# A hybrid decoder layer: decay sums by a scan instead of products, regrouped masked products, and 512-column products in the feed-forward part

## Chip, core, metric

One core of one Trainium2 chip runs the whole layer. The metric is the device time of one execution in microseconds (us). Before the change the median of 3 runs is 466.96 us (466.77 to 468.04).

## What is computed

The layer has one batch of 256 tokens and 1024 channels, all in fp32. Cut to what matters:

```python
h = rms_norm(x, norm1_g);  proj = h @ w_in                 # 1024 -> all mixers and gates
# mixer A (RWKV-7, 8 heads x 64); p is the token-shifted part of proj
w_log = -softplus(-(w0 + tanh(xw) @ w_up)) - 0.5
decay = exp(-exp(w_log))                                   # = exp(-exp(-0.5) * sigmoid(w0 + ...))
a = sigmoid(a0 + xa @ a_up)
kk = heads(k * k_k);  kk = kk / max(norm(kk), 1e-12)       # norm over the 64 channels of a head
k = k * (1 + (a - 1) * k_a)
def step(S, (r, w, k, v, -kk, kk*a)):                      # 256 steps, S is 64 x 64 per head
    sa = S @ a_t
    S = S * w_t + outer(sa, b_t) + outer(v_t, k_t)
    return S, S @ r_t
# group norm, bonus sum(r*k*r_k)*v, gate g; mixer B: causal attention; mixer C: causal pooling
x = x + sum(gates * branch, axis=2) @ w_out
h2 = rms_norm(x, norm2_g)
x = x + square(relu(h2 @ w_ff1)) @ w_ff2                   # 1024 -> 4096 -> 1024
```

The recurrence is computed in blocks: products of decayed keys, queries and values inside a block, the inverse of a triangular matrix by levels of doubling, and a state that is carried from block to block. The factors exp(+sum) and exp(-sum) of the running sums of log decay are what turns the step-wise decay into such products.

## The kernel before

**Units and slots.** All large products are cut into 69 units (`UNITS`, lines 57 to 68), and every engine runs one loop over slots t = 0 to 68, unit t being computed in slot t. A unit has two weight pieces of 128x1024 elements (`PIECES` = 138, piece v belongs to unit v // 2). "feat" units (0 to 6, 13, 14) and "ff1" units have channels on the output's partitions: weights stationary, activations moving, 256 columns (tokens) a product. "tok", "branch", "out" and "ff2" units have tokens on partitions and move 512 columns of weights. From slot 37 on ff1 and ff2 units alternate, 16 of each.

**fp32 by halves.** Each operand is a high part (type fp32r) and a rest, and a product is three (`mm3`, lines 496 to 499): high x high (L497), then the two mixed ones (L498, L499). In a feat or ff1 unit these are 16 x 3 products of 256 columns.

**The weight pipeline.** SyncE (SP) loads piece v into one of 3 stages (L470) once DVE has finished low(v - 3). ScalarE (ACT) casts it to the high part, high(v) (L900), once PE has used piece v - 6. VectorE (DVE) subtracts, low(v) (L1142). PE waits for low(v). `split_places` gives the pieces to the slots: slot 2 has 7, 8 and 9; slot 3 has 10 and 11; slot 4 has 12, 13 and 14; slot 5 has 15 and 16; slot 6 has 17 and 18; slot 7 has 19 and 20; slot 8 has 21 and 22; slot 9 has 23 and 24.

**Order inside a slot.** A slot has four parts p on PE; after part p of the unit PE runs `extra(t, p)`, the small products placed at (t, p). ACT and DVE run their own extra(t, p) in the order 0 to 3 between the high(v) or low(v) of the slot, then `finish(t)` (the unit's result out of PSUM) before extra(t, 3). On ACT slot 3 begins with extra(3, 2). Each engine's order is fixed by this text; a wait in one step holds all behind it on that engine. For t < 7, finish(t) mixes each token with its predecessor: ACT L1068, DVE L1401. Unit t of these uses PSUM bank `FEAT_BANK[t]`; unit 6 uses the bank of unit 4, so PE's part (6, 0) waits for DVE's finish(4).

**Decay.** At (2, 1) PE makes z = tanh(xw) @ w_up with tokens on partitions (L647) and the product for a (L652). DVE, first thing in slot 2, adds w0, which was broadcast to all partitions by a load (`decay_input`, L1178). ACT (2, 1) takes four sigmoids of 256 columns for a (L927) and two of 512 for z (L930). At (3, 2) and (4, 0) PE multiplies the sigmoids by a triangular constant `C_CUM` (`cum`, L663), which gives the running sums of a chunk of 128 tokens, taken from its middle; ACT takes exp of them with both signs (L936, L937) into `e_up` and `e_dn`.

**Norms of kk.** DVE (3, 0) multiplies k by k_k (L1185), ACT (3, 2) squares (L941), PE (4, 1) sums over heads (L671), DVE (4, 1) takes the maximum (L1189), GpSimd (POOL) the root (L1472, once per call), ACT (4, 3) spreads it (`kkb`, L944), PE (5, 2) transposes it, DVE (5, 3) multiplies.

**Products and inverse.** DVE (4, 2) makes k2 (L1195, L1197); (5, 2), (6, 0) and (6, 3) multiply keys and queries by the exponentials; (7, 0) ends with `ops_ready`. `PROD_AT` places four groups of masked products: (8, 0) and (8, 2) for chunk 0, (9, 0) and (9, 2) for chunk 1, each 16 pairs of 64x64 tiles on PE (L626, L629), drained with a mask by DVE (L1246, two of 128x512 a group). Then DVE (8, 3) and (9, 3) builds the start of the inverse (L1255, L1261), and PE transposes it, X0, at (9, 1) for chunk 0 and (10, 1) for chunk 1 (L722). The first level of the inverse is PE's (11, 0) (L743). The bonus product (L706) is at (8, 1), drained by DVE (L1237).

**State.** The state is carried over four steps of 64 tokens, `s_bd`; since sums run from a chunk's middle, it is rescaled once, at n == 1 (L1305).

**Feed-forward.** ff1(i) has one PSUM bank with two halves of 256 columns. In its own slot ACT takes Relu (L1097) and Square into the high part `r_hi` (L1101); DVE squares (L1428) and subtracts into `r_lo` (L1431, the helper at L1146). ff2(i) waits for that; it stands two units behind ff1(i).

Of the kernel before, what the change touches and what calls it, by code (L numbers as in the profile page):

```python
# [28 lines left out]
P = 128  # L29
# [9 lines left out]
WINDOWS = (2, 4, 8, 16)  # L39
PAD = 16  # L40
# [4 lines left out]
C_ID, C_BLK, C_CUM, C_BIAS = 0, 128, 256, 386  # L45
# [31 lines left out]
PROD_AT = {(8, 0): (0, 0), (8, 2): (0, 1), (9, 0): (1, 0), (9, 2): (1, 1)}  # L77
# [44 lines left out]
def plan_turns():  # L122
# [14 lines left out]
    for t, u in enumerate(UNITS):  # L137
# [4 lines left out]
        for p in range(4):  # L142
            if p == 0:
# [37 lines left out]
def pe_uses(t, p):  # L181
# [3 lines left out]
    if (t, p) == (3, 2):  # L185
        return [(("cum", 0, 0),), (("cum", 0, 1),)]
    if (t, p) == (4, 0):
        return [(("cum", 1, 0),), (("cum", 1, 1),)]
# [9 lines left out]
    if (t, p) == (8, 1):  # L198
# [3 lines left out]
    if (t, p) in PROD_AT:  # L202
        out += [(("prod", *PROD_AT[t, p], e),) for e in range(2)]
# [35 lines left out]
    if h2_place(t, p) is not None:  # L239
        out += [(("h2", 2 * h2_place(t, p) + i),) for i in range(2)]  # L240
# [3 lines left out]
def dense_ends():  # L244

    ends = {}
    for t, u in enumerate(UNITS):
# [9 lines left out]
        if u[0] == "ff1":  # L257
            ends[("ff", u[1])] = 2 * t + 2
# [6 lines left out]
def build_layer(nc: bass.Bass, x, w_in, w_up, w0, a_up, g_up, pool_w, w_branch, w_out, w_ff1, w_ff2, vecs, consts, out):  # L265
    turn = plan_turns()
    ctx = ExitStack()
    with ctx:
# [3 lines left out]
        def sem(name):  # L272
# [6 lines left out]
        h_hi = sb("h_hi", [P, KD, T], F32R)  # L279
        h_lo = sb("h_lo", [P, KD, T], F32R)  # L280
# [17 lines left out]
        small = sb("small", [P, 96])  # L298
# [10 lines left out]
        sg = big[:, 2].rearrange("p (t n) -> p t n", t=TT)  # L309
# [4 lines left out]
        e_up, e_dn = (flat[:, 4096 + 1040 * i:4096 + 1040 * i + 1032].rearrange("p (c j t) -> p c j t", c=TT, j=PAIRS)  # L314
                      for i in range(2))
# [22 lines left out]
        w0_wide = att[:, 0:512]  # L338
# [6 lines left out]
        e_end, minus_half = small[:, 48:52], small[:, 52:53]  # L345
# [47 lines left out]
        def copied(eng, name):  # L393
# [6 lines left out]
        id_in, vec_in, cst_in, mask_in, small_in, w0_in, g_in, pool_in = (  # L400
            sem(n) for n in ("id_in", "vec_in", "cst_in", "mask_in", "small_in", "w0_in", "g_in", "pool_in"))
# [9 lines left out]
        keep_part, sg_ready = sem("keep_part"), sem("sg_ready")  # L411
# [15 lines left out]
        f_hi, f_ready = sem("f_hi"), sem("f_ready")  # L427
# [35 lines left out]
        def _(sp):  # L463
# [3 lines left out]
            for v in range(PIECES):  # L467
# [27 lines left out]
        def _(pe):  # L495
# [37 lines left out]
            def part(t, p):  # L533
# [6 lines left out]
                if u[0] in ("feat", "ff1"):  # L540
# [1031 lines left out]
```

## Time and profile before

| | us |
|---|---|
| median of 3 runs | 466.96 |
| profiled execution, its own time | 467.01 |
| its span | 465.2 |
| PE busy | 459.6 |
| PE weight loads busy | 397.7 |
| DVE busy | 295.0 |
| ACT busy | 245.8 |

The span is the profiled time between the first and the last instruction of the core; 1.8 us lie around it. PE's records overlap, since a product is drained while the next one begins: the time that a product costs is the distance between two starts, not its own duration. In a timeline row the first column is the start, the second the time till the end of the last record of the row, "x4" says how many records it merges, and the bracket says how long the engine was idle before and what ended that.

### The profile page before, as it was taken

The numbers are of one execution on the slowest core, as the hardware profiler recorded it, in microseconds if no ns is written. First come the engines' busy times: TensorE is split into PE (matmuls) and PEld (weight loads), VectorE is DVE, ScalarE is ACT, GpSimd is POOL, SyncE is SP. The second block draws the span as 40 slices with busy tenths as digits, with TensorE's granted clock in tenths as the row PEclk, the third lists the DMA queues.
The fourth block names the chain that finished last, engine by engine and source line by source line (L and its number), as shares of the span: only waits on it lengthen the run. The fifth ranks groups of instructions, "written<-read, shape, count | busy, mean of one in ns | idle before, by whom it ended". The sixth has DMA issues, their size and how long they took to land.

```text
span 465.2 us, 8736 instructions
## 1 busy us (share of the span) xinstructions
PE 459.6 (99%) x3660; PEld 397.7 (85%) x3660; DVE 295.0 (63%) x405; ACT 245.8 (53%) x370; POOL 33.1 (7%) x41
## 2 busy tenths in 40 slices
PE   8999999999999999999999999999999999999997
PEld 4999986788977778788888889999999999999995
DVE  4675998674564766766778758655555555555542
ACT  5597655646555456566543538444444444444430
POOL 2000100021670001002000000000000000000000
PEclk9999999999999999999999999999999999999999
DMA  7776635533424435445656564655556656565602
GB/s 235 235 231 217 220 96 177 151 122 93 145 87 136 118 110 142 130 159 171 189 185 184 175 193 143 209 184 184 184 189 194 197 184 182 185 182 190 204 10 90
DMA packets 48694, 76.91 MB, mean 165 GB/s; under 512 B 2576, under 2 KB 28944, under 8 KB 48656
## 3 DMA queue, kind: packets, MB, share of 16 engines
q1 hardware_dynamic: 48656, 76.36, 53.1%
q8 instruction: 29, 0.48, 0.4%
q14 instruction: 9, 0.07, 0.0%
HBM read 75.30 MB, written 1.05 MB: 164 GB/s over the span
## 4 chain that ended last, share of the span: by engine, by line
PE 90%; DVE 3%; ACT 2%; DMA 2%; issue 1%; POOL 1%; DVEq 0%; ACTq 0%
PE bank L497 26%; PE bank L498 25%; PE bank L499 25%; DMA stage<-in_w_in 2%; PE bank L606 1%; PE bank L762 1%; PE bank L743 1%; DVE w_lo L1142 1%; PE bank L638 1%; ACT w_hi L900 1%; POOL small L1472 1%; DVE xs L1458 1%; PE bank L626 1%; PE bank L829 1%; PE bank L793 1%
## 5 line engine op out<-in xcount | busy, mean ns | idle before, releaser
L1142 DVE TENSOR_TENSOR w_lo<-stage,w_hi 128x1024 fp32r<-128x1024 f32 x138 | 167.9, 1225 | 89.1 <-ACT w_hi L900 89.1
L900 ACT CAST w_hi<-stage 128x1024 fp32r<-128x1024 f32 x138 | 144.5, 1052 | 109.5 <-PE bank L499 88.6
L497 PE MATMUL bank<-h_hi,w_hi 128*128 128x256 f32 x384 | 109.8, 286 | 0.3 <-DVE h_lo L1386 0.3
L498 PE MATMUL bank<-h_lo,w_hi 128*128 128x256 f32 x384 | 108.6, 283 | 0.0
L499 PE MATMUL bank<-h_hi,w_lo 128*128 128x256 f32 x384 | 108.6, 283 | 0.0
L497 PEld LDWEIGHTS bank<-h_hi,w_hi 128*128 128x128 f32 x384 | 73.6, 192 | 1.6 <-issue 0.8
L498 PEld LDWEIGHTS bank<-h_lo,w_hi 128*128 128x128 f32 x384 | 73.6, 192 | 0.6
L499 PEld LDWEIGHTS bank<-h_hi,w_lo 128*128 128x128 f32 x384 | 73.6, 192 | 0.0
L497 PE MATMUL bank<-w_hi,h_hi 128*128 128x512 f32 x144 | 60.4, 420 | 0.0
L497 PE MATMUL bank<-w_hi,r_hi 128*128 128x512 f32 x144 | 56.4, 392 | 0.0
L499 PE MATMUL bank<-w_hi,h_lo 128*128 128x512 f32 x144 | 56.4, 391 | 0.0
L498 PE MATMUL bank<-w_lo,h_hi 128*128 128x512 f32 x144 | 56.4, 391 | 0.0
L498 PE MATMUL bank<-w_lo,r_hi 128*128 128x512 f32 x144 | 56.2, 390 | 0.0
L499 PE MATMUL bank<-w_hi,r_lo 128*128 128x512 f32 x144 | 56.0, 389 | 0.0
L497 PEld LDWEIGHTS bank<-w_hi,h_hi 128*128 128x128 f32 x144 | 27.0, 188 | 7.7 <-issue 2.4
L499 PEld LDWEIGHTS bank<-w_hi,h_lo 128*128 128x128 f32 x144 | 27.0, 188 | 6.1
L499 PEld LDWEIGHTS bank<-w_hi,r_lo 128*128 128x128 f32 x144 | 27.0, 188 | 5.8
L497 PEld LDWEIGHTS bank<-w_hi,r_hi 128*128 128x128 f32 x144 | 27.1, 188 | 5.2
L498 PEld LDWEIGHTS bank<-w_lo,r_hi 128*128 128x128 f32 x144 | 27.1, 188 | 4.9
L498 PEld LDWEIGHTS bank<-w_lo,h_hi 128*128 128x128 f32 x144 | 27.1, 188 | 4.7 <-issue 0.2
L1472 POOL TENSOR_TENSOR small<-small 128x8 f32<-128x8 f32 (+2 forms) x9 | 15.0, 1676 | 173.7 <-DVE small L1320 69.1
L1097 ACT ACTIVATE mat<-bank 128x512 f32<-128x512 f32 x16 | 9.6, 599 | 30.5 <-PE bank L499 30.5
(231 smaller groups left out, 541.9 us busy)
## 6 DMA issues: line engine op xcount, KB each, us to landing
stage<-in_w_ff SPq DMA_DIRECT2D x64, 512.0 KB, 3.8
stage<-in_w_in SPq DMA_DIRECT2D x54, 512.0 KB, 3.8
stage<-in_w_branch SPq DMA_DIRECT2D x12, 512.0 KB, 4.5
stage<-in_w_out SPq DMA_DIRECT2D x8, 512.0 KB, 4.1
xs<-in_x SPq DMA_DIRECT2D x2, 512.0 KB, 3.9
out<-xs SPq DMA_DIRECT2D x4, 256.0 KB, 2.1
cst<-in_consts SPq DMA_DIRECT2D x1, 608.0 KB, 6.6
att<-in_w SPq DMA_DIRECT2D x1, 256.0 KB, 5.9
```

The costliest lines, as they stand in the source:

```text
L497: pe.matmul(o, lh, rh, start=first, stop=False)
L498: pe.matmul(o, lh, rl, start=False, stop=False)
L499: return pe.matmul(o, ll, rh, start=False, stop=last)
L606: pe.matmul(banks[3][:], flat[:, 0:P], flat[:, 0:512], start=True, stop=True)
L626: ins = pe.matmul(o[halves[e], P * i:P * i + P], bk[c][halves[e], j, s, 0:HD], ar[c][halves[e], j, :, HD * s:HD * s + HD], start=True, sto ...
L638: ins = pe.transpose(o[:, P * j:P * j + P], x_c[:, c, j].rearrange("p s n -> p (s n)"), ident)
L743: ins = pe.matmul(both[e][halves[s], HD * i:HD * i + HD], gm[c][halves[e], j, s, e, 0:HD], x_c[halves[e], c, j, s], start=True, stop=True)
L762: ins = pe.matmul(both[s][halves[e], HD * i:HD * i + HD], left, right, start=True, stop=True)
L900: nc.scalar.copy(w_hi[:, v % RING], stage[:, v % STAGES]).then_inc(hi_done, 1)
L1097: nc.scalar.activation(ffs[i % 2], o[:], ACT.Relu).then_inc(drained_of(("ff", i)), 1)
L1142: dve.tensor_tensor(w_lo[:, v % RING], stage[:, v % STAGES], w_hi[:, v % RING].bitcast(F32), ALU.subtract)\
L1472: pool.tensor_tensor(ap, ap, half.to_broadcast(shape), ALU.pow).then_inc(done, 1)
```

## The change

1. **Decay.** z is made with channels on partitions (four products of 256 columns at (2, 1), interleaved with those for a). w0 is loaded as four columns (`w0_col`, 4-byte elements, ahead of a_up on SP's queue) and added by ACT as the bias of the sigmoid, which writes into segments of 1 + 64 (`SEG`), the first element of each being 0. One `tensor_tensor_scan` on DVE over 1040 elements (`sum_decay`, in slot 3 behind extra(3, 0)) gives the running sums, restarted in every block of 64 tokens. Two exponentials of 1040 on ACT (3, 2), now between high(10) and high(11), replace eight of 258 columns. The products `cum` and `C_CUM` go.
2. **Norms earlier.** ACT squares at (3, 1), first thing in slot 3; DVE takes the maximum at (3, 1), between low(10) and low(11); ACT spreads the root at (4, 0), first thing in slot 4. PE's sum stays at (4, 1).
3. **Products regrouped.** The two groups of a chunk stand together: (8, 2) and (9, 2). The bonus moves from (8, 1) to (10, 0).
4. **State.** With sums per block of 64 the state is rescaled in each of the steps n = 0, 1 and 2 by its own factor.
5. **Feed-forward.** `h_hi` and `h_lo` become one tile `h_two`; high weights times both are one product of 512 columns into a bank of its own half-unit, the rest of the weights times `h_hi` one of 256 into its second half. DVE adds the halves (two `tensor_reduce`), then max(x, 0) * x in one instruction; ACT copies to `r_hi` at (t + 1, 0) and DVE subtracts at (t + 1, 1).
6. ACT clears `zz` at (6, 3) instead of (7, 2).

```diff
-PROD_AT = {(8, 0): (0, 0), (8, 2): (0, 1), (9, 0): (1, 0), (9, 2): (1, 1)}
+PROD_AT = {(8, 2): 0, (9, 2): 1}
+BONUS_AT = (10, 0)
...
                 elif u[0] == "ff1":
-                    use(("ff", u[1]), dense=True)
+                    for j in range(2):
+                        use(("ff", u[1], j), 6 - 2 * (u[1] % 2) + j, dense=j == 1)
...
                     sp.dma_start(lora[0:64, 0], w_up[0]).then_inc(small_in, 16)
+                    sp.dma_start(w0_col, w0[0].rearrange("(j p) -> p j", p=P), allow_slow_non_contiguous=True).then_inc(small_in, 16)
                     sp.dma_start(lora[64:128, 1], a_up[0]).then_inc(small_in, 16)
-                    sp.dma_start(w0_wide, w0[0].partition_broadcast(P)).then_inc(w0_in, 16)
...
+                if u[0] == "ff1":
+                    name = ("ff", u[1], i)
+                    o = room(pe, name) if p < 2 else ps(name)
+                    cols = slice(P * i, P * i + P)
+                    for kk in range(4):
...
+                        pe.matmul(o[:].rearrange("p (s t) -> p s t", s=2), wh[:, kk, cols], h_two[:, :, k],
+                                  start=k == 0, stop=False)
+                        ins = pe.matmul(o[:, T:2 * T], wl[:, kk, cols], h_hi[:, k], start=False, stop=k == KD - 1)
...
-                if (t, p) in ((3, 2), (4, 0)):
-                    c = t - 3
...
-                            ins = pe.matmul(o[:, 256 * jj:256 * jj + 129], sg[:, c, P * j:P * j + P],
-                                            cst[:, C_CUM:C_CUM + 129], start=True, stop=True)
...
                 if (t, p) in PROD_AT:
-                    products(*PROD_AT[t, p])
+                    for g in range(2):
+                        products(PROD_AT[t, p], g)
...
+                            ins = nc.scalar.activation(sg[:, :, j, :, 1:SEG], o[:, T * jj:T * jj + T].rearrange("p (c s t) -> p c s t", c=TT, s=2),
+                                                       ACT.Sigmoid, bias=w0_col[:, j:j + 1])
...
-                if (t, p) == (3, 2):
+                if (t, p) == (3, 1):
                     act.wait_ge(kkraw_ready, 1)
                     nc.scalar.activation(ksq, kkn, ACT.Square).then_inc(ksq_ready, 1)
-                if (t, p) == (4, 3):
+                if (t, p) == (3, 2):
+                    act.wait_ge(cum_ready, 1)
+                    nc.scalar.activation(e_up_all, cum_all, ACT.Exp, scale=-DECAY).then_inc(e_ready, 1)
+                    nc.scalar.activation(e_dn_all, cum_all, ACT.Exp, scale=DECAY).then_inc(e_ready, 1)
+                if (t, p) == (4, 0):
                     act.wait_ge(kk_inv, 1)
...
+                if p == 0 and UNITS[t - 1][0] == "ff1":
+                    i = UNITS[t - 1][1]
+                    act.wait_ge(sq_ready, i + 1)
...
             for t in range(SLOTS):
                 step = (t, 2) in STEP_AT or (t, 3) in STEP_AT
                 if t == 3:
-                    extra(t, 2)
-                if step:
+                    extra(t, 1)
+                if step or t == 4:
                     extra(t, 0)
                 for v in split_places(2 * t):
                     high(v)
-                if not step:
+                if not step and t != 4:
                     extra(t, 0)
                 late = t in (S_OUT - 1, S_FF - 1)
                 if t == 2 or step:
                     extra(t, 1)
+                if t == 3:
+                    extra(t, 2)
                 for v in () if late else split_places(2 * t + 1):
                     high(v)
...
+            def sum_decay():
+
+                dve.wait_ge(seg_ready, 2)
                 for i in range(2):
...
+                    copied(dve, ("z", i))
+                dve.tensor_tensor_scan(cum_all, restart, sg_all, 0.0, ALU.mult, ALU.add).then_inc(cum_ready, 1)
...
-                if (t, p) == (8, 1):
+                if (t, p) == BONUS_AT:
...
+                    for g, e in ((0, 0), (0, 1), (1, 0), (1, 1)):
                         name = ("prod", c, g, e)
...
+                            ins = dve.tensor_tensor(s_bd[rows, :, e], by_pair(o[rows, 0:PAIRS * HD]),
+                                                    e_end[rows, 0, :, 0:1].to_broadcast([HD, PAIRS, HD]), ALU.mult)
...
+                if p == 1 and UNITS[t - 1][0] == "ff1":
+                    i = UNITS[t - 1][1]
+                    b = 2 * (i % 2)
+                    dve.wait_ge(f_hi, i + 1)
...
+                    for j in range(2):
+                        o = take(dve, ("ff", i, j))
+                        dve.tensor_reduce(ffs[i % 2][:, T * j:T * j + T], o[:].rearrange("p (s t) -> p t s", s=2), AX_X, ALU.add)\
+                           .then_inc(drained_of(("ff", i, j)), 1)
...
+                    dve.scalar_tensor_tensor(out=fsq[i % 2], in0=ffs[i % 2], scalar=0.0, in1=ffs[i % 2],
+                                             op0=ALU.max, op1=ALU.mult).then_inc(sq_ready, 1)
...
             for t in range(SLOTS):
-                if t == 2:
-                    decay_input()
                 extra(t, 0)
+                if t == 3:
+                    sum_decay()
                 for v in split_places(2 * t):
                     low(v)
```

## Rows read from the trace of the kernel before

**Rows 1.** The page: busy times, granted clock, costly groups (L606 from the groups by line).

```profile
PE 459.6 (99%) x3660; PEld 397.7 (85%) x3660; DVE 295.0 (63%) x405; ACT 245.8 (53%) x370; POOL 33.1 (7%) x41
...
PEclk9999999999999999999999999999999999999999
...
L900 ACT CAST w_hi<-stage 128x1024 fp32r<-128x1024 f32 x138 | 144.5, 1052 | 109.5 <-PE bank L499 88.6
...
L606 PE MATMUL bank<-mat 128*128 128x512 f32 x8 | 6.8, 1027 | 1.4 <-DVE mat L1148 1.4
```

**Rows 2.** The waits: who waited for whom, us in total, times, longest.

```profile
ACT w_hi L900 <- PE bank L499: 88.6, 70, 2.5
```

**Rows 3.** PE's timeline: starts of ff1(2), ff2(1) and ff1(3).

```profile
299.25 0.28 PE L497 MATMUL bank<-h_hi,w_hi 128*128 128x256 f32 x1
...
305.00 0.40 PE L497 MATMUL bank<-w_hi,r_hi 128*128 128x512 f32 x1
...
310.47 0.28 PE L497 MATMUL bank<-h_hi,w_hi 128*128 128x256 f32 x1
```

**Rows 4.** PE's timeline, slots 3 to 11: the small products and what follows them.

```profile
34.34 1.05 PE L663 MATMUL bank<-cst,big 128*128 128x129 f32 x8
35.15 0.36 PE L497 MATMUL bank<-h_hi,w_hi 128*128 128x256 f32 x1
...
53.42 0.28 PE L497 MATMUL bank<-h_hi,w_hi 128*128 128x256 f32 x1
...
67.01 0.33 PE L626 MATMUL bank<-ops 64*64 64x128 f32 x2
...
68.05 0.50 PE L497 MATMUL bank<-w_hi,h_hi 128*128 128x512 f32 x1
...
69.54 1.02 PE L706 MATMUL bank<-att,cst 128*128 128x512 f32 x2
...
71.30 0.80 PE L497 MATMUL bank<-w_hi,h_hi 128*128 128x512 f32 x1
...
79.71 0.60 PE L722 MATMUL bank<-cst,mat 128*128 128x128 f32 x4
...
92.90 0.29 PE L743 MATMUL bank<-mat 64*64 64x64 f32 x4
```

**Rows 5.** DVE's timeline, slots 3 to 8.

```profile
35.01 1.14 DVE L1185 TENSOR_SCALAR mat<-big,vec 128x256 f32<-128x256 f32 x4
...
48.05 1.38 DVE L1195 TENSOR_SCALAR mat<-mat,vec,small 128x256 f32<-128x256 f32 x4
...
50.61 0.87 DVE L1401 SCALAR_TENSOR_TENSOR big<-bank,vec,big 128x255 f32<-128x255 f32 x2
51.86 1.22 DVE L1142 TENSOR_TENSOR w_lo<-stage,w_hi 128x1024 fp32r<-128x1024 f32 x1 [0.39 <-ACT w_hi L900]
...
67.10 2.36 DVE L1142 TENSOR_TENSOR w_lo<-stage,w_hi 128x1024 fp32r<-128x1024 f32 x2
...
76.46 1.29 DVE L1255 TENSOR_TENSOR mat<-mat,cst 128x512 f32<-128x512 f32 x2
77.78 1.72 DVE L1261 TENSOR_TENSOR mat<-mat,cst 64x256 f32<-64x256 f32 x4
```

**Rows 6.** ACT's timeline, slots 2 and 3.

```profile
29.32 0.84 ACT L927 ACTIVATE mat<-bank,vec 128x256 f32<-128x256 f32 x2
...
31.80 1.06 ACT L900 CAST w_hi<-stage 128x1024 fp32r<-128x1024 f32 x1
32.74 0.86 ACT L1068 ACTIVATE big<-bank,small 128x256 f32<-128x256 f32 x2
33.62 1.28 ACT L936 ACT_TABLE_LOAD   x1
34.99 0.39 ACT L936 ACTIVATE mat<-bank 128x258 f32<-128x258 f32 x1
```

**Rows 7.** The loads of L470 from 60 to 80 us: time from issue to landing.

```profile
DMA to landing us min/median/max: 3.6/3.7/4.8
```

More of the change, by code:

```diff
@@ L202, in pe_uses @@
     if (t, p) in PROD_AT:
-        out += [(("prod", *PROD_AT[t, p], e),) for e in range(2)]
+        out += [(("prod", PROD_AT[t, p], g, e),) for g in range(2) for e in range(2)]
     if (t, p) in FIRST_X_AT:
@@ L239, in pe_uses @@
     if h2_place(t, p) is not None:
-        out += [(("h2", 2 * h2_place(t, p) + i),) for i in range(2)]
+        out += [(("h2", 2 * h2_place(t, p) + i), 4 + i) for i in range(2)]
     return out
@@ L308, in build_layer @@
         pool_sb = big[:, 5, 0:512].rearrange("p (g d) -> p g d", g=4)
-        sg = big[:, 2].rearrange("p (t n) -> p t n", t=TT)
+        restart, sg_all, cum_all = (ops[:, PAIRS * CHUNKS * SEG * i:PAIRS * CHUNKS * SEG * (i + 1)] for i in range(3))
+        segs = lambda z: z.rearrange("p (c j s t) -> p c j s t", c=TT, j=PAIRS, t=SEG)
+        sg = segs(sg_all)
         xn = big[:, 4:6]
@@ L922, in extra @@
                 if (t, p) == (2, 1):
+                    act.wait_ge(small_in, 48)
+                    act.wait_ge(seg_ready, 2)
+                    for i in range(2):
+                        o = take(act, ("z", i))
+                        for jj in range(2):
+                            j = 2 * i + jj
+                            ins = nc.scalar.activation(sg[:, :, j, :, 1:SEG], o[:, T * jj:T * jj + T].rearrange("p (c s t) -> p c s t", c=TT, s=2),
+                                                       ACT.Sigmoid, bias=w0_col[:, j:j + 1])
+                        ins.then_inc(drained_of(("z", i)), 1)
                     for i in range(2):
@@ L1052, in extra @@
                         ins.then_inc(h2_hi, 1)
+                if p == 0 and UNITS[t - 1][0] == "ff1":
+                    i = UNITS[t - 1][1]
+                    act.wait_ge(sq_ready, i + 1)
+                    if i >= 2:
+                        act.wait_ge(used, 2 * (UNITS.index(("ff2", i - 2)) + 1))
+                    nc.scalar.copy(r_hi[:, 2 * (i % 2):2 * (i % 2) + 2], fsq[i % 2].rearrange("p (k t) -> p k t", k=2))\
+                      .then_inc(f_hi, 1)
                 if (t, p) == (S_FF, 1):
@@ L1091, in finish @@
                       .then_inc(drained_of(("unit", t)), 1)
-                elif u[0] == "ff1":
-                    i = u[1]
-                    if i >= 2:
-                        act.wait_ge(f_ready, i - 1)
-                    o = take(act, ("ff", i))
-                    nc.scalar.activation(ffs[i % 2], o[:], ACT.Relu).then_inc(drained_of(("ff", i)), 1)
-                    copied(act, ("ff", i))
-                    if i >= 2:
-                        act.wait_ge(used, 2 * (UNITS.index(("ff2", i - 2)) + 1))
-                    nc.scalar.activation(r_hi[:, 2 * (i % 2):2 * (i % 2) + 2], ffs[i % 2].rearrange("p (k t) -> p k t", k=2),
-                                         ACT.Square).then_inc(f_hi, 1)
             for t in range(SLOTS):
@@ L1116, in _ @@
                     extra(t, 1)
+                if t == 3:
+                    extra(t, 2)
                 for v in () if late else split_places(2 * t + 1):
                     high(v)
-                if t != 2 and not step:
+                if t not in (2, 3) and not step:
                     extra(t, 1)
```

144 lines of the change are left out of this document (60 added, 84 removed).

## Prediction, made before the change was run

> **What bounds the kernel now.** I read the page first: TensorE (PE) is busy for 459.6 of 465.2 us and its granted clock is full in every slice [rows 1]. So the first question is not which engine is short, but what the change takes off PE's stream and whether PE will have to wait for what feeds it. The list of waits says the same from the other side: ACT's casts of the weights wait 88.6 us for PE to free a buffer, so weights are ahead of it [rows 2]. Then I read PE's timeline [rows 3, 4], those of VectorE (DVE) [rows 5] and ScalarE (ACT) [rows 6], and the time that a load takes to land [rows 7]. In the feed-forward part PE runs without a gap. In slots 3 to 9 it hardly waits either, but there DVE has no idle moment from low(15) at 51.86 to the end of low(20), 67.10 + 2.36 [rows 5] (the instructions between are back to back), and X0 of chunk 0, the transposed start of the inverse, is issued at 79.71 [rows 4], 0.2 us after DVE's last instruction for it ended (77.78 + 1.72) [rows 5]. PE and DVE are balanced to a fraction of a us at that point.
>
> **The base.** The sum is made against the profiled execution: span 465.2, its own time 467.0, which is the median of the runs (466.96).
>
> **Feed-forward products.** A ff1 unit of 48 products of 256 columns takes 305.00 - 299.25 = 5.75 us, 0.120 each. The ff2 unit of 24 products of 512 columns takes 310.47 - 305.00 = 5.47, 0.228 each [rows 3]. A new ff1 unit has 16 products of 512 and 16 of 256: 16 x (0.228 + 0.120) = 5.56, 0.19 less; 16 units give **-3.0 us**. The 512-column product now reads two runs of 256 instead of one run, which no row shows. Bounds: it costs as much as the two it replaces (gain 0), or 512 columns at 2.4 GHz with nothing on top, 0.213 (gain 256 x 0.026 = 6.7). I take the ff2 row, the nearest. DVE gets two sums out of PSUM and one product (0.64 to 0.69 each: two of that size take 1.29 [rows 5]), ACT one copy. After the end of a ff1 unit stand one sum, the product, ACT's copy, and the rest: some 2.8 us, beside a low(v) up to 4. What needs them is the unit after the next one, and the one between lasts 5.47 at least. Without that cover the whole 4 us would be paid in each of 16 units. Cost 0.
>
> **Decay sums on PE.** The two groups of `cum` products go: 35.15 - 34.34 = 0.81 us each [rows 4], -1.62 on PE's stream before unit 6. The z products are cut in two but run beside the a products on the other half of the rows: 0. The w0 columns replace a 256 KB broadcast by 512 elements of 4 bytes, in the same place of SP's queue, ahead of the loads of a_up and of piece 6; PE's and ACT's (2,1) wait for them instead of DVE. No row shows such a load. Between a load of 512 KB (3.6 to 4.8 [rows 7]) and one that is 1 us slower than the broadcast was, it costs 0 to +1; I take 0, since it moves 2 KB. In slots 17 to 21 DVE gets one more product of the state, 0.7 us, four parts of PE ahead of its use: 0.
>
> **The chain that replaces them**, times as in the profile of before:
> 1. ACT's (2,1) gets eight sigmoids of 128x256. Two take 0.84 with the next begun at 0.72, so 2.9 us, where 31.80 - 29.32 = 2.5 lie now before high(9) [rows 6]. Everything behind, to the end of DVE's kkn, comes 0.4 later: 36.55 instead of 35.01 + 1.14 = 36.15 [rows 5].
> 2. ACT's order is then: the square (moved ahead of high(10)), high(10), the table load 1.28, two exponentials of 1040, high(11). A pass of ACT over 1024 takes 1.05, the next starts 0.1 sooner [rows 1], so they end at 37.6, 38.6, 39.9, 41.9, 42.9. DVE's scan lies beside the square and high(10). No row shows a scan. Its bounds are one pass over 1024 (1.22 [rows 5]) and two (2.5), done at 37.8 or 39.1, both before the table load ends, so either costs 0. Whether the load stands ahead of the exponentials, as at 33.62 now, or earlier and hidden, decides 0.7 us at the end; I take the first.
> 3. low(11) ends at 44.15. It used to be early; now load(14) is issued on it. Landing 3.7 [rows 7], high(14), low(14), k2 (50.61 - 48.05 = 2.56), finish(4) 0.87 [rows 5]: 47.9, 48.95, 50.15, 52.7, 53.6.
> 4. PE arrives at unit 6, whose bank finish(4) drains, at 53.42 [rows 4] - 1.62 = 51.8 and waits till 53.6. **The 1.62 us are given back here**, and a little more.
> 5. From there DVE has no idle time to make it up: low(15) moves from 51.86 to 53.5, low(19) from 67.10 to 68.75 [rows 5].
> 6. load(22) is issued when low(19) ends, 70.0, lands at 73.7; high(22) and low(22) end at 75.9. The merged products put all four drains of chunk 0 behind low(22): 4 x 0.62 = 2.5 (their size is that of the pair at 76.46, 1.29 for two), where two of them and the bonus used to fill DVE's waits before it. Then the inverse's start, 79.50 - 76.46 = 3.04 [rows 5]: done at **81.4**.
> 7. PE comes to X0 of chunk 0 earlier than now. From unit 6 to it were 79.71 - 53.42 = 26.3; the bonus (71.30 - 69.54 = 1.76), the third product group (68.05 - 67.01 = 1.04) and about 0.5 of broken-up parts leave [rows 4]: 23.0. From 53.6 it arrives at 76.6, or 77.1 with a short wait for finish(6), and waits about 4.6 us.
> 8. X0 at 81.45 against 79.71 is +1.75. Behind it now lie the bonus (+1.7) and one more product group (+0.9, its 0.16 of entry shared), which used to be ahead: the first level, 92.90 now [rows 4], starts at 97.25. **+4.35 us** (+3.65 with the table load hidden). The levels, steps and attention after it move as a block, since weights are ahead there [rows 2].
>
> Two interruptions of the stream fewer are worth 0.3 to 0.7 us, but the one in chunk 0 falls into the wait.
>
> Sum: 467.0 + 4.35 - 3.0 = 468.35, **468.4 us**.
>
> **A rule weighed.** The table load's row begins at 33.62, and the exponential at 34.99, 0.09 us after its end; the activation before it ended as it began [rows 6]. So the switch costs 1.28 by the trace, as used in step 2. The Trainium skill (ScalarE: Activation LUTs, What ACT_TABLE_LOAD costs) gives 2.66 us for a switch, the load and a drain. By that page step 2 and so the sum would end 1.4 later, 469.8; this trace doesn't show the drain, and I give it no chance of its own.
>
> **Rivals.**
> - *The clock falls in the wait of step 7.* Now PE is idle for 5.6 us in all, nearly all of it at the two ends, and the granted clock is full [rows 1]. The first eight records of 512 columns, from 1.44 to 8.04 us, take 0.83 us each [rows 1], and the four of the bonus 0.43 [rows 4]: half speed after idleness is in the trace, though the clock row doesn't mark it. If a wait of 4.6 us brings it back for as much work as those eight records hold, 8 x 0.43 = 3.4 us, that work takes twice as long: up to +3.4, and with a shorter stretch +1 to +2; some 470.7 us. The Trainium skill (TensorE: Matmul & The Clock Gate, Part 1) states this rule: an idle TensorE is put back to 1.2 GHz, and only sustained work releases it. Chance 0.22.
> - *Faster: DVE is in time at X0 of chunk 0.* Its place is step 6. It decides when the inverse's start is done before PE's arrival near 77, so if steps 2 to 6 together take 4.6 us less than I reckon (loads that land sooner, low(v) that no longer wait). Then only what leaves PE counts: -1.6 - 0.7 - 3.0, 461.7 us; half of it gives 465. For it speaks that DVE loses two sums over 512 columns; against it, that steps 3 and 6 each hold a load's landing that starts from a low(v), and no idle DVE lies between. Chance 0.18.
> - *The 512-column products bring nothing* (two runs read, or PSUM reads of DVE in the way), the early loss stays: 467.0 + 4.35 = 471.4. Chance 0.10.
>
> **The numbers.** The forecast's own case has 0.50, by its bounds 467.4 to 469.6. A measurement of this kernel can tell 0.3%, 1.4 us: 468.4 lies just at that bound, so half of the case counts as the same. Slower: 0.25 + 0.22 + 0.10 = 0.57; same 0.25; faster 0.18. The range reaches up to the third rival, 471.4, and down to 464.5, half-way into the faster one; what it leaves out is the rest of that and a clock that falls for longer.
>
> **What would show it.** In the profile of after: PE idle for 4 to 5 us right before X0 of chunk 0 (near 77 to 81), released by DVE's masked copies of the inverse's start; a shorter wait before unit 6, released by finish(4); low(11) near 43, low(22) near 75, the first level at 97; a ff1 unit of 5.56 us; the granted clock full, or halved for a stretch behind the wait. Wrong would be: the first level at or before 92.9 (then steps 2 to 6 are too long), no PE wait at X0, or a ff1 unit still at 5.75.

## The result and the profile after

The changed kernel took 471.95 us (median of 4 runs, 471.52 to 473.10), the kernel before 467.24 in the same comparison; the ratio is 1.010 (95% interval 1.008 to 1.012). The forecast was 468.4 with a range up to 471.4: slower was right, the size too small, and the measured time lies just outside the range. The profiled execution of after took 471.97, with a span of 469.8, where before had 467.01 and 465.2: 4.6 us more in the span, and 0.35 us more around it.

The page of the kernel after, its busy times and the granted clock in 40 slices of 11.7 us:

```profile
PE 457.7 (97%) x3392; PEld 384.7 (82%) x3392; DVE 313.6 (67%) x437; ACT 237.5 (51%) x350; POOL 34.1 (7%) x44
...
PEclk9999899899999999999999999999999999999999
```

Against [rows 1], PE is busy 1.9 us less in a span 4.6 us longer, so it is idle 6.5 us more. Two slices have lost clock, the fifth and the eighth. The waits of PE in the kernel after (who waited for whom, us in total, times, longest):

```profile
PE bank L725 <- DVE mat L1263: 3.6, 1, 3.6
PE bank L500 <- DVE big L1410: 3.0, 1, 3.0
PE bank L620 <- DVE mat L1152: 1.4, 1, 1.4
```

The first is X0 of chunk 0 waiting for the inverse's start (L1263 is L1261 of before), the second unit 6 waiting for finish(4). Both were forecast, at 4.6 and 1.8 us. PE's timeline of the kernel after shows both waits, the bonus, the first level and two ff1 pairs:

```profile
54.36 0.55 PE L500 MATMUL bank<-h_two,w_hi 128*128 128x256 f32 x1 [3.02 <-DVE big L1410]
55.14 0.41 PE L500 MATMUL bank<-h_two,w_hi 128*128 128x256 f32 x1
...
58.72 0.28 PE L500 MATMUL bank<-h_two,w_hi 128*128 128x256 f32 x1
...
82.04 1.11 PE L725 MATMUL bank<-cst,mat 128*128 128x128 f32 x4 [3.59 <-DVE mat L1263]
82.81 0.78 PE L500 MATMUL bank<-w_hi,h_two 128*128 128x512 f32 x1
...
88.04 0.40 PE L500 MATMUL bank<-w_hi,h_two 128*128 128x512 f32 x1
...
90.99 1.45 PE L708 MATMUL bank<-att,cst 128*128 128x512 f32 x3
...
99.20 0.99 PE L746 MATMUL bank<-mat 64*64 64x64 f32 x52
...
305.43 0.39 PE L551 MATMUL bank<-h_two,w_hi 128*128 128x512 f32 x1
305.66 0.28 PE L553 MATMUL bank<-h_two,w_lo 128*128 128x256 f32 x1
305.77 0.40 PE L551 MATMUL bank<-h_two,w_hi 128*128 128x512 f32 x1
...
311.07 0.40 PE L500 MATMUL bank<-w_hi,r_hi 128*128 128x512 f32 x1
```

Against [rows 4]: unit 6 starts 0.9 later, X0 2.3 later, the first level 6.3 later. Against [rows 3], a ff1 unit takes 311.07 - 305.43 = 5.64, where 5.75 stood; 16 of them give back 1.8, and 6.3 - 1.8 makes the span's 4.6 to within 0.1. The record of a product of 512 columns lasts 0.78 behind the wait and 0.40 later. The windows of PE's stretches (columns: window, length, busy time and count of PE, its weight loads, DVE, ACT and POOL, granted clock, DMA share, GB/s):

```profile
54.00:56.00 2.00, 1.64 (x8) 1.68 (x9) 2.00 (x3) 2.00 (x4) 0.00 (x0) 0.54 0.03 12
56.00:58.00 2.00, 2.00 (x12) 2.00 (x12) 2.00 (x5) 0.46 (x1) 0.00 (x0) 0.61 0.74 197
58.00:60.00 2.00, 2.00 (x19) 2.00 (x18) 1.90 (x5) 1.03 (x1) 0.00 (x0) 1.00 0.87 306
...
80.00:82.00 2.00, 0.00 (x0) 0.00 (x0) 1.91 (x5) 0.00 (x0) 0.00 (x0) 0.87 0.00 0
82.00:84.00 2.00, 1.96 (x7) 1.77 (x8) 1.99 (x2) 0.59 (x1) 0.00 (x0) 0.50 0.00 0
84.00:86.00 2.00, 2.00 (x29) 1.44 (x31) 0.38 (x1) 0.00 (x0) 0.00 (x0) 0.78 0.66 181
```

A granted clock of 0.50 is the level of 1.2 GHz, and a value between 0.50 and 1.00 says in which part of its window the clock was low. So PE works at 1.2 GHz from 54.4 to about 57.6 and from 82.0 to about 84.9. Since 2.8 us at half speed hold 1.4 us of work, the second stretch should cost about 1.4 us; the first makes PE only later at X0, where it waits anyway. That is a reading so far, and run e6 tests it.

DVE's and ACT's timelines of the kernel after carry the chain:

```profile
36.74 2.32 DVE L1182 TENSOR_TENSOR_SCAN ops<-ops 128x1040 f32<-128x1040 f32 x1
38.87 1.28 ACT L946 ACT_TABLE_LOAD   x1
40.16 1.07 ACT L946 ACTIVATE mat<-ops 128x1040 f32<-128x1040 f32 x1
43.16 1.23 DVE L1146 TENSOR_TENSOR w_lo<-stage,w_hi 128x1024 fp32r<-128x1024 f32 x1 [2.91 <-ACT w_hi L903]
48.57 1.05 ACT L903 CAST w_hi<-stage 128x1024 fp32r<-128x1024 f32 x1 [1.87 <-DMA stage<-in_w_in]
...
53.34 0.87 DVE L1410 SCALAR_TENSOR_TENSOR big<-bank,vec,big 128x255 f32<-128x255 f32 x2
54.12 2.35 DVE L1146 TENSOR_TENSOR w_lo<-stage,w_hi 128x1024 fp32r<-128x1024 f32 x2
...
74.33 1.05 ACT L903 CAST w_hi<-stage 128x1024 fp32r<-128x1024 f32 x1 [1.48 <-DMA stage<-in_w_in]
75.42 1.23 DVE L1146 TENSOR_TENSOR w_lo<-stage,w_hi 128x1024 fp32r<-128x1024 f32 x1 [1.31 <-ACT w_hi L903]
76.56 2.47 DVE L1248 TENSOR_TENSOR mat<-bank,cst 128x512 f32<-128x512 f32 x4
80.27 1.72 DVE L1263 TENSOR_TENSOR mat<-mat,cst 64x256 f32<-64x256 f32 x4
```

The reader can follow the forecast's steps here: the scan (nobody waits for it), the table load right ahead of the exponential, low(11) at 43.16, high(14), finish(4) to 54.21, low(15), high(22), low(22), four drains in a row, the start of the inverse done at 81.99.

### The profile page after: what moved, and what is told of

It is laid out like the page before. It is cut to its first block, busy times and chain, and to the rows that moved or that the text cites. A ratio compares the mean times of both kernels' runs of the same rounds, so it can differ in the third digit from the quotient of the medians.

```text
span 469.8 us, 8199 instructions
## 1 busy us (share of the span) xinstructions
PE 457.7 (97%) x3392; PEld 384.7 (82%) x3392; DVE 313.6 (67%) x437; ACT 237.5 (51%) x350; POOL 34.1 (7%) x44
## 4 chain that ended last, share of the span: by engine, by line
PE 81%; DVE 8%; DMA 5%; ACT 3%; issue 2%; SPq 0%; DVEq 0%; ACTq 0%
PE bank L500 18%; PE bank L501 17%; PE bank L502 17%; PE bank L551 13%; PE bank L553 6%; DMA stage<-in_w_in 5%; DVE w_lo L1146 2%; ACT w_hi L903 2%; PE bank L746 1%; PE bank L765 1%; PE bank L652 1%; DVE xs L1469 1%; PE bank L832 1%; DVE h_two L1168 1%; PE bank L796 1%
## 5 line engine op out<-in xcount | busy, mean ns | idle before, releaser
L551 PE MATMUL bank<-h_two,w_hi 128*128 128x512 f32 x256 | 91.2, 399 | 0.3 <-DVE h_two L1389 0.3
L553 PE MATMUL bank<-h_two,w_lo 128*128 128x256 f32 x256 | 71.8, 281 | 0.0
L500 PE MATMUL bank<-w_hi,h_two 128*128 128x512 f32 x144 | 60.8, 422 | 0.0
L551 PEld LDWEIGHTS bank<-h_two,w_hi 128*128 128x128 f32 x256 | 48.1, 188 | 12.3 <-issue 0.6
L501 PE MATMUL bank<-w_lo,h_two 128*128 128x512 f32 x144 | 56.7, 394 | 0.0
L502 PE MATMUL bank<-w_hi,h_two 128*128 128x512 f32 x144 | 56.6, 393 | 0.0
L553 PEld LDWEIGHTS bank<-h_two,w_lo 128*128 128x128 f32 x256 | 48.3, 189 | 0.6
L500 PE MATMUL bank<-h_two,w_hi 128*128 128x256 f32 x128 | 37.9, 296 | 3.0 <-DVE big L1410 3.0
L501 PE MATMUL bank<-h_two,w_hi 128*128 128x256 f32 x128 | 36.8, 288 | 0.0
L502 PE MATMUL bank<-h_two,w_lo 128*128 128x256 f32 x128 | 36.7, 287 | 0.0
L500 PEld LDWEIGHTS bank<-w_hi,h_two 128*128 128x128 f32 x144 | 27.3, 190 | 7.5 <-issue 2.1
L502 PEld LDWEIGHTS bank<-w_hi,h_two 128*128 128x128 f32 x144 | 27.3, 189 | 6.2
L501 PEld LDWEIGHTS bank<-w_lo,h_two 128*128 128x128 f32 x144 | 27.4, 190 | 4.9 <-issue 0.2
L500 PEld LDWEIGHTS bank<-h_two,w_hi 128*128 128x128 f32 x128 | 25.2, 197 | 3.7 <-issue 3.5
```

Of the source, the lines that this page charges most:

```text
L500: pe.matmul(o, lh, rh, start=first, stop=False)
L501: pe.matmul(o, lh, rl, start=False, stop=False)
L502: return pe.matmul(o, ll, rh, start=False, stop=last)
L551: pe.matmul(o[:].rearrange("p (s t) -> p s t", s=2), wh[:, kk, cols], h_two[:, :, k], start=k == 0, stop=False)
L553: ins = pe.matmul(o[:, T:2 * T], wl[:, kk, cols], h_hi[:, k], start=False, stop=k == KD - 1)
```

## The experiments

Some runs of a kernel fall to 1.2 GHz for a stretch and others do not; where a span "at full clock" is given, it is the median of the runs with a mean clock of at least 0.999. Ratios are to the kernel before, timed in turn with the run on the same chip, and differences of spans at full clock are to the same median of the kernel before in that comparison: 465.65 for e1 to e4, 465.6 for e5 to e8, 465.2 for e9 to e12. Places in a trace are set against the one profiled run of before (span 465.2).

**Theory.** The loss is made ahead of the inverse. DVE, not PE, times X0, so PE's work taken from ahead of it earns nothing, and what is put behind it costs in full; the clock's fall behind the wait adds about 1.4; the feed-forward part earns less than forecast. Where an expectation has a theory A, it is what this says of that run. **Rivals:** something in the changed feed-forward part gives time back; the decay part's chain makes X0 late by itself; the clock's fall is harmless.

### The feed-forward part alone (e1), its operands in one run of memory (e2), its products in blocks (e8)

e1 is the kernel before with part 5 alone. e2 adds:

```diff
-        h_two = sb("h_two", [P, 2, KD, T], F32R)
-        h_hi, h_lo = h_two[:, 0], h_two[:, 1]
+        h_two = sb("h_two", [P, KD, 2, T], F32R)
+        h_hi, h_lo = h_two[:, :, 0], h_two[:, :, 1]
```

> The kernel before with part 5 of the change alone (512-column high products, the halves added on DVE). Theory A (what the trace after shows: a pair of products of 512 and 256 columns starts every 0.353 us where the sum took 0.348): 16 units of 5.65 in place of 5.75, so 1.6 to 1.7 us faster than before, ratio about 0.9965. Theory B (the recorded sum: the gain is 3.0 us and something in the changed feed-forward part, such as a wait for the adding on DVE or the later high part, gives back 1.3): still 1.7 faster by time, but with waits of PE in the feed-forward slots that the trace names. Theory C (the front part's stalls in the changed kernel took something from it): 3.0 us faster, ratio 0.9936.

> As the run with the feed-forward part alone, but h_two is laid out [partition, k, half, token], so that the 512 columns are one run of memory and not two of 256 that lie apart. If the 5 ns a pair above the sum is the read of two runs: pairs of 0.348, 0.08 us a unit less, 1.3 us faster than the run with the feed-forward part alone. If it is the change between products of 512 and of 256 columns (or of their weights): pairs stay at 0.353 and the time is the same within 0.3 us.

Measured: e1 465.52, ratio 0.995 (0.993 to 0.997), e2 465.66, ratio 0.996 (0.995 to 0.998). A ff1 unit is 5.64 in both, as in the changed kernel. Theory A holds for e1: 1.7 us less span in the trace (463.5 against 465.2), 1.95 by the spans at full clock, and no wait of PE in the feed-forward part that before did not have. The interval of the ratio alone would leave room for theory C's 0.9936; the measured unit does not. Two runs of memory are not the price.

e8 takes e1 and issues the products of a part in blocks:

```diff
                         pe.matmul(o[:].rearrange("p (s t) -> p s t", s=2), wh[:, kk, cols], h_two[:, :, k],
                                   start=k == 0, stop=False)
+                    for kk in range(4):
+                        k = 4 * (p // 2) + kk
                         ins = pe.matmul(o[:, T:2 * T], wl[:, kk, cols], h_hi[:, k], start=False, stop=k == KD - 1)
```

> The kernel before with the feed-forward part alone, and in it the four products of 512 columns of a part first, then the four of 256, in place of one by one. If the 5 ns a pair come from the alternation, eight products take 4 x 0.228 + 4 x 0.120 = 1.39 us, a unit 5.57, 1.3 us faster than the feed-forward part alone (464.2). If a product of 512 moving columns of activations simply costs 0.235 after any other: no difference within 0.3 us (465.5). A third possibility: a short product is paid in full by its own weight load only behind another short one (the mean distance of 0.120 before against 0.118 in the pairs), then 0.1 us slower a unit, 467.

PE's timeline of e8, a ff1 unit's blocks and the start of the ff2 unit behind:

```profile
301.56 1.07 PE L550 MATMUL bank<-h_two,w_hi 128*128 128x512 f32 x4
302.47 0.64 PE L554 MATMUL bank<-h_two,w_lo 128*128 128x256 f32 x4
302.94 1.09 PE L550 MATMUL bank<-h_two,w_hi 128*128 128x512 f32 x4
...
307.15 0.40 PE L499 MATMUL bank<-w_hi,r_hi 128*128 128x512 f32 x1
```

Four products of 512 take 302.47 - 301.56 = 0.91, 0.228 each, four of 256 take 0.47, 0.118 each; the unit is 307.15 - 301.56 = 5.59. In the changed kernel, where the two kinds alternate, the next start comes 0.236 behind a product of 512 and 0.117 behind one of 256 (means over some 250 of each in the trace). So the forecast's 0.228 was the price of a product of 512 among its like, and one that alternates with shorter ones costs 0.236. The blocks bring 0.8 us over 16 units, of which ff2 units give 0.3 back (5.49 in place of 5.47); the time is 465.28, ratio 0.996 (0.994 to 0.997), which can't be told from e1's. The profiled run of e8 is its longest (span 465.5, the median at full clock is 463.45), and its trace says why:

```profile
11.29 1.66 PE L516 MATMUL bank<-h_two,w_hi 128*128 128x256 f32 x8 [1.90 <-ACT h_two L927]
```

Behind this wait of 1.9 us near the kernel's start, where e8 and e1 are the same, the granted clock was 0.50 until about 15.6, and the first level of the inverse came 2.2 later than in e1 (95.22 against 92.99). So a run without a trace whose mean clock is 0.996 may have lost its clock there; 4 of the 26 runs of the kernel before that were timed with e1 to e4 have 0.996 too, with spans of 467.7 to 468.4.

### The products regrouped (e3), and its two halves (e9, e10)

e3 is the kernel before with part 3 alone; e9 keeps the bonus at (8, 1); e10 moves the bonus only.

```diff
-PROD_AT = {(8, 0): (0, 0), (8, 2): (0, 1), (9, 0): (1, 0), (9, 2): (1, 1)}
+PROD_AT = {(8, 2): 0, (9, 2): 1}
+BONUS_AT = (10, 0)
```

> The kernel before with part 3 of the change alone: products of a chunk together at (8, 2) and (9, 2), the bonus at (10, 0). Theory A (the four drains and the start of the inverse come after the second part of slot 8, so X0 at (9, 1) waits whatever the front does): PE waits 2 to 4 us for DVE ahead of X0, and 1.5 to 4 us slower than before, more if the clock falls behind the wait. Theory B (the lateness at X0 comes from the decay and norm part, which makes low(19) to low(22) late; the regrouping alone is covered): within 0.8 us of before.

> The kernel before with the product groups of a chunk put together at (8, 2) and (9, 2), the bonus left at (8, 1). Theory A (X0 is timed by DVE, so what is taken from PE ahead of it is only paid again behind it): two drains that used to lie in DVE's idle time ahead of low(21) now lie behind low(22), X0 1.2 us later, and PE's group of 1.05 us from (9, 0) comes behind X0: 2.2 us slower, span 467.4, time about 469.3. Theory B (regrouping is free, the bonus costs it all): within 0.5 us of before.

> The kernel before with the bonus at (10, 0) and nothing else changed. Theory A: X0 stays where DVE has it (79.7, at most 0.5 earlier), PE waits for it 1 to 1.5 us, and the bonus of 1.5 us comes behind it: 1.0 to 1.3 us slower, time about 468.5. With the groups' 2.2 it makes the 3.4 us of the run with both. Theory B (PE is what times X0, and the bonus is the same work at another place): within 0.4 us of before.

Measured: e3 471.87, ratio 1.009 (1.006 to 1.013); e9 468.89, ratio 1.004 (1.002 to 1.005); e10 467.98, ratio 1.002 (1.000 to 1.003). In spans at full clock: 468.6 (one run), 466.8 and 466.0, that is +3.0, +1.6 and +0.8. PE's timelines, first e3's X0 and first level:

```profile
80.42 0.66 PE L724 MATMUL bank<-cst,mat 128*128 128x128 f32 x4 [3.56 <-DVE mat L1262]
...
96.27 1.16 PE L745 MATMUL bank<-mat 64*64 64x64 f32 x64
```

then the same two in e9:

```profile
80.64 0.66 PE L724 MATMUL bank<-cst,mat 128*128 128x128 f32 x4 [0.98 <-DVE mat L1262]
...
94.77 1.16 PE L745 MATMUL bank<-mat 64*64 64x64 f32 x64
```

In e3 X0 comes only 0.7 later than in [rows 4], but the first level comes 3.4 later: PE has waited 3.56 us for DVE ahead of X0, and then does behind it what it used to do before it. DVE's timeline of e3 shows why DVE can't be earlier, since it waits where a group's drain used to lie, and the drains come behind low(22):

```profile
72.36 1.23 DVE L1144 TENSOR_TENSOR w_lo<-stage,w_hi 128x1024 fp32r<-128x1024 f32 x1 [2.21 <-ACT w_hi L902]
73.79 1.23 DVE L1144 TENSOR_TENSOR w_lo<-stage,w_hi 128x1024 fp32r<-128x1024 f32 x1 [0.20 <-ACT w_hi L902]
...
77.33 1.28 DVE L1256 TENSOR_TENSOR mat<-mat,cst 128x512 f32<-128x512 f32 x2
```

Theory A is confirmed for e3 and e9, though e9's cost is 1.6 and not 2.2, its X0 is 0.9 later and not 1.2, and most of PE's waiting is elsewhere: 2.35 us ahead of the product groups at (8, 2), where their bank waits for DVE to drain the bonus, and 0.98 ahead of X0. e10's median fits theory A, but its full-clock spans run from 464.9 to 467.1, and in its profiled run (464.9) X0 came at 77.65, 2.1 us earlier; "X0 stays" was wrong for that run. DVE's timelines show both reasons, first before's, then e10's:

```profile
72.93 1.28 DVE L1237 TENSOR_TENSOR vmix<-bank,vmix 128x512 f32<-128x512 f32 x2
```

```profile
70.86 2.58 DVE L1143 TENSOR_TENSOR w_lo<-stage,w_hi 128x1024 fp32r<-128x1024 f32 x2 [0.86 <-ACT w_hi L901]
```

In before the drain of the bonus lies between low(21) and low(22). It is work of DVE ahead of X0, and moving the bonus takes it away, which gives about 1.1 us; the other 0.9 is a high(21) that ended sooner (low(21) at 70.86, where before has 71.79). The two halves make 2.4 of the 3.0, and e3's 3.0 is that of one run, so whether anything comes from their meeting can't be told. The other three runs of e3, at a mean clock of 0.993 to 0.995, have spans of 469.5 to 471.0.

### The decay part alone (e4), and the changed kernel with the products as before (e5)

e4 is the kernel before with parts 1, 2, 4 and 6. e5 is the changed kernel with part 3 undone, so e4 and the feed-forward part.

> The kernel before with parts 1, 2, 4 and 6 of the change alone (scan, norms, state, zz), products and bonus where they were. Theory A (chain of finish(4)): PE waits about 3 us at the start of unit 6 and gives back the 1.6 us of the products cum that are gone, its clock may fall to 1.2 GHz behind that wait; slots 7 to 9 give it nothing back, so 1 to 2.5 us slower than before. Theory B (the products alone are late at X0, the wait at unit 6 is paid for by cum): 0 to 0.5 us slower. The sum of this run's difference and that of the products alone tells whether the two parts meet: 4.6 + 1.7 = 6.3 us is what the changed kernel lost ahead of the first level of the inverse.

> The changed kernel with part 3 undone: four product groups at (8, 0), (8, 2), (9, 0), (9, 2) and the bonus at (8, 1), as before. Theory A (parts add up): the decay part cost 1.1 us of span alone, the feed-forward part gave 1.7, so a span of 464.6 and a time of about 466.8 (2.15 around the span, as in the two kernels with the scan), 5.2 us faster than the changed kernel; no wait at X0. Theory B (the chain from finish(4) makes X0 late however the products stand): a wait of 2 us or more at X0 stays and the time is 469 or more.

Measured: e4 468.99, ratio 1.002 (1.001 to 1.004), span at full clock 466.3; e5 467.34, ratio 1.000 (0.999 to 1.001), median span 465.2. The wait at unit 6 is 2.4 in e4 and 2.2 in e5, and neither waits at X0:

```profile
PE bank L499 <- DVE big L1396: 2.4, 1, 2.4
PE bank L608 <- DVE mat L1143: 1.4, 1, 1.4
```

(waits of e4). X0 starts at 80.70, 1.0 later than in [rows 4], and the first level at 93.92, also 1.0 later. So the decay part, which takes 1.6 us of products off PE, costs 1.0 by its trace and 0.6 by the spans at full clock. For e5 theory A's 466.8 was 0.5 too low: 465.2 of span, not 464.6. In 6 of e5's 10 runs the mean clock was 0.995 or 0.996, in the profiled one by a stretch behind unit 6's wait; their median span is 465.65, that of the other 4 is 465.2. In e4, whose profiled run kept its clock, 6 of 10 runs have 0.996 and a median of 467.15, against 466.25 of the others. Where the clock fell in the runs without a trace isn't known.

In the profiled runs the first level of the inverse is 3.4 later in e3, 1.0 in e4 and 0.1 in e1 (92.99), together 4.5. In the changed kernel it is 6.3 later. What is left is 1.8. The spans at full clock are +3.0, +0.6 and -1.95, together +1.6, where the changed kernel's profiled run has +4.6; with e3's only such run in it, this sum is the weaker one.

### The two waits filled (e6)

```diff
                     c = FIRST_X_AT[t, p]
+                    o = room(pe, ("X0", c))
+                    for _ in range(14 if c == 0 else 0):
+                        pe.matmul(o[:], h_hi[:, 0, 0:P], h_hi[:, 0:2], start=True, stop=True)
                     pe.wait_ge(xt_ready, c + 1)
-                    o = room(pe, ("X0", c))
```

and 12 such products ahead of unit 6, into the bank of unit 2.

> The changed kernel, with products that nobody reads put into its two long waits of PE: 12 of 512 columns ahead of unit 6 (into the bank of unit 2) and 14 ahead of X0 for chunk 0 (into X0's own bank, before it is written); no result changes. 12 x 0.228 = 2.7 us into the wait of 3.0, 14 x 0.228 = 3.2 us into the wait of 3.6. If the fall of the clock behind the waits costs 1.35 us: granted clock at 1.00 throughout (the run's mean 0.999 or 1.000 where the changed kernel has 0.993), no slices at 0.50, time 470.6. If the fall costs nothing (DVE sets the pace behind X0 too): clock up, time 471.9. If the filling is too long or is itself in the way: 472.5 or more.

Measured: 470.61, ratio 1.006 (1.004 to 1.008), spans 468.2 to 468.9, mean clock 0.999 to 1.000 in all four runs. PE's stretches in e6, to be set against the same windows of the changed kernel:

```profile
82.00:84.00 2.00, 2.00 (x18) 1.47 (x20) 2.00 (x2) 0.59 (x1) 0.00 (x0) 1.00 0.00 0
84.00:86.00 2.00, 2.00 (x65) 1.80 (x58) 1.14 (x3) 0.00 (x0) 0.00 (x0) 1.00 0.88 232
```

X0 starts at 81.80 and the first level at 97.64, 15.84 apart, where the changed kernel has 17.16. Products that nobody reads made the kernel 1.34 us faster by the medians, and the stretch behind X0 alone is 1.32 shorter: the fall of the clock costs what was read from the trace. X0 itself moved by 0.24, the most that the first fall can have cost. The first level is now 4.7 later than in [rows 4], where the parts make 4.5: at that place they add up but for 0.3. By the spans at full clock they don't: e6 has 468.45, +2.85, the parts make +1.6, and these 1.25 us are open. Part of it can be the reference, since the profiled run of before, at 465.2, was 0.4 shorter than the median of before in the comparisons of e1 to e8.

### Unit 6 not held up: another bank (e7), finish(4) first (e11), and with the rest undone (e12)

e7 has `FEAT_BANK` with 6: 2 in place of 6: 0. e11 has, in DVE's slot 4:

```diff
-                extra(t, 2)
+                if t != 4:
+                    extra(t, 2)
                 finish(t)
+                if t == 4:
+                    extra(t, 2)
```

e12 is e5 with this and with e8's blocks.

> The changed kernel with unit 6 in PSUM bank 2 (drained since unit 2) and not in bank 0, so that its first product no longer waits for DVE's finish(4). Theory A (DVE's order of work sets X0): the 3.0 us of wait are gone at unit 6, but X0 for chunk 0 starts within 0.5 us of 82.0 as in the changed kernel, PE's wait there grows to about 5 to 6.5 us, and the time is 471 to 472.5. Theory B (PE's late start of unit 6 is what makes the ring of weight pieces, low(19) to low(22) and so X0 late): X0 moves up by 1.5 to 3 us and the time to 469 to 470.5.

> The changed kernel with DVE's finish(4) ahead of k2 (4, 2), 2.5 us earlier. Theory A (DVE's order behind X0's chain decides): the wait of 3.0 us at unit 6 falls to below 1, with it the first fall of the clock; k2 is done when it was, low(15) and low(16) too, so X0 starts within 0.5 us of 82.0 and the wait there grows to 5 to 6.5 us; time 471 to 472.5. Theory B (the wait at unit 6 is a loss of its own): 1.5 to 3 us faster than the changed kernel, 469 to 470.5.

> The changed kernel with part 3 undone (products and bonus as before), finish(4) ahead of k2, and the feed-forward products in blocks of four. Run e5 had 465.2 of span at full clock with a wait of 2.2 at unit 6. If that wait is a loss of its own: 463 of span, 465.2. If X0 is timed by DVE: the wait moves to X0, 464.4 to 465.2 of span, 466.6 to 467.3, and the kernel with the feed-forward part alone (465.3 to 465.5) stays the fastest.

Measured: e7 473.48, ratio 1.012 (1.009 to 1.016); e11 471.59, ratio 1.009 (1.007 to 1.011); e12 467.22, ratio 1.000 (0.999 to 1.001). e7's bank was badly chosen: unit 7 uses bank 2, so it had to wait 7.4 us for DVE's finish(6), and the run tells only that the wait can move; X0 fell to 84.73, which neither theory had. e11 and e12 have no such side effect. The waits of e11:

```profile
PE bank L725 <- DVE mat L1263: 3.5, 1, 3.5
PE bank L702 <- issue: 2.2, 1, 2.2
```

The wait at unit 6 is gone; one of 2.2 us stands at (7, 3) instead, where PE's transposes of v (L702) need DVE's finish(6) (it ends at 65.14, they start at 65.24), and X0 starts at 81.75, 0.3 earlier than in the changed kernel. In e12 it is 2.5 us at the same place:

```profile
64.90 1.06 PE L704 MATMUL bank<-cst,vmix 128*128 128x128 f32 x8 [2.49 <-issue]
```

Theory A holds in the time and in X0's place; where the wait goes, it had wrong: not to X0 but to the next thing that DVE hands over. In these kernels DVE is the bound from slot 5 to X0, and PE's slack shows up wherever the two meet.

### Around the span (e13, e14)

e13 is e1 with the load of w0 as columns added. e14 is e5 without that load and without the bias of the sigmoid, so it leaves w0 out of what it computes.

> The kernel with the feed-forward part alone, and the load of w0 as four columns added at the same place on SP's queue, into a place that nobody reads. If the load of 512 elements of 4 bytes makes the 0.35 us outside the span: time minus span 2.15 (1.83 without it), 465.9. If not: 1.8 and 465.5.

> The changed kernel with the products undone (465.2 of span, 2.1 to 2.2 around it), with w0 left out: no load of it, and the sigmoid without bias. If the load makes the 0.35 us: time minus span 1.8, 467.0. If the scan or something else of the decay part makes it: 2.15 and 467.3.

Time minus span: 1.77 in e13 (465.92), 2.16 in e14 (467.01), medians over 8 and 10 runs. The times fall on the numbers of the theory that blames the load, but by luck of the spans; the quantity in question doesn't: it is not the load. All kernels with the decay part have 2.15 to 2.2 and all without it 1.76 to 1.82; what in it makes the 0.35 us is open.

## Why the prediction was right in direction and short in size

**Right.** The forecast's direction and its path, steps 1 to 6: the sum's own times against after are low(11)'s end 44.15 (44.39), finish(4)'s 53.6 (54.2), low(19) 68.75 (69.36), low(22)'s end 75.9 (76.65), the inverse's start 81.4 (81.99). The cum products' 1.62 us were given back at unit 6, as said. The scan took 2.32 us, within its bounds of 1.22 and 2.5, beside the square and high(10), at no cost. The table load stood ahead of the exponentials and cost 1.28: they begin at 40.16, 0.01 after its end. The Trainium skill's 2.66 for a switch (ScalarE: Activation LUTs, What ACT_TABLE_LOAD costs) is again not seen. The load of the w0 columns kept nobody waiting at (2, 1): PE reaches it at 24.64, where before has 25.13. The medians of e13 and e14 would allow it 0.3 to 0.4 us (465.92 against e1's 465.52, 467.01 against e5's 467.34), no more than single runs of one kernel differ by. What DVE and ACT got more in the feed-forward part cost nothing (e1).

**Wrong: "Feed-forward products", 16 x (0.228 + 0.120).** -3.0 was -1.8 by the units (16 x 0.11), -1.7 by e1's profiled span and -1.95 by its spans at full clock. The price of a 512-column product was read from a row where it follows its like; in alternation with 256-column ones it is 0.236 (e8 against e1). The unit was 5.64, not 5.56. The bounds, 0 and 6.7, hold it; in blocks the unit is 5.59.

**Mis-sized: steps 3 to 8, +4.35.** It measured 6.3, 1.95 more. Of this 0.6 was there at X0 already (82.04, not 81.45): low(11) ended 0.24 late, and high(14) began 4.2 us after that end where 3.7 was taken for the load of piece 14 (the row gave 3.6 to 4.8), which DVE, without idle time from low(15) to low(20), passed on. The rest, 1.35, lies between X0 and the first level, and is the clock: the sum put its fall at nothing.

**The first rival happened.** The forecast gave "the clock falls in the wait" 0.22 as an exclusive case; in the profiled run of after it fell behind X0's wait and already behind unit 6's, and the mean clock of the other three, 0.992 or 0.993, is as low. Its price, +1 to +2 with a shorter stretch, was right: 1.34 by e6. The rule of the Trainium skill that was cited there (TensorE: Matmul & The Clock Gate, Part 1), that an idle TensorE is put back to 1.2 GHz, agrees with this trace (0.50 behind both waits); e3's profiled run, at full clock behind a wait of 3.56 us, shows that it doesn't happen each time. Adding the price to the forecast's own case instead of setting it beside would have given 468.35 + 1.34 = 469.7, with the measured feed-forward gain 470.9, and with the late load and the 0.35 around the span 471.9.

**Not in the sum:** 0.35 us around the span, with the decay part; its cause is open.

The third rival's 471.4 lies nearer to the measured time than the forecast does, but by luck: its premise, that the 512-column products bring nothing, didn't hold (1.8 us).

Step 7's arrival of PE at X0 (76.6 to 77.1) was 78.45, since unit 6 began 0.8 later than reckoned and then ran at half clock (in e6, at full clock, PE arrives at 77.08), and so the wait was 3.6 and not 4.6. The fastest versions tried are the kernel before with the feed-forward part alone, one by one or in blocks: e1 is 0.995 (0.993 to 0.997) of before, and 0.986 of the changed kernel by the medians (465.52 and 471.95).

## What to carry to other kernels

When another engine times a meeting point, work that the bound-looking engine sheds ahead of it earns nothing and work moved behind it costs its whole length: look for the next hand-over before counting a removal. Count what the timing engine sheds or gets as well: the bonus took its drain along (e10). A forecast wait of some us on TensorE should carry the price of the clock, with its chance, in the same case, not as a separate one. The distance between two products is a property of the pair: take it from rows with the same neighbour.

## What the runs showed of the hardware

- In the profiled runs the clock fell to 1.2 GHz behind waits of PE of 1.9 us (e8), 2.2 (e5, e11), 2.5 (e12), 3.0 and 3.6 (after), 3.5 (e11) and 7.4 (e7), but not behind waits of 2.35 (e9), 2.4 (e4) and 3.56 us (e3). So the length of the wait alone doesn't decide it. The fall can come when PE is at work again: in e12 the clock was full until about 66.3, 1.4 us after PE had resumed at 64.90.
- While the clock was low PE worked for 2.8 us (after, from 82.0 to 84.9), 3.2 us (after, from 54.4 to 57.6) and 4.7 us (e7, from 65.9 to 70.6).
- Products that nobody reads, in waits that exist anyway, were worth 1.34 us (e6).
- Behind a product of 512 columns in fp32r the next starts after 0.228 us among its like and after 0.236 where it alternates with products of 256; one of 256 takes 0.117 to 0.120 in either place.
- Two reads of 256 columns lying apart cost a moving operand nothing against one run of 512 (5.64 a unit in both).
- A scan over 1040 columns of fp32 took 2.32 us on DVE, where a product of two tensors over 1024 takes 1.23.
